# One decoder layer on one core: attention units in another order, outputs rounded one step earlier

## Chip, core and metric

The kernel runs on one core of one Trainium2 chip. The metric is the device time of one execution in microseconds. The core has five engines, each with an instruction queue of its own that is worked off strictly in order: TensorE (PE: matmuls and transposes), VectorE (DVE), ScalarE (ACT), GpSimd (POOL) and SyncE (SP, which only issues DMAs here). They wait for each other through semaphores: an instruction that ends adds to a counter, another engine's queue stands still until the counter has reached a number.

## What is computed

One layer of a decoder trunk on 512 tokens of width 1024. The change touches only the attention of the "native sparse" branch. Of the reference, cut to that part (16 heads of 64 channels, 4 key/value heads):

```python
def _nsa_branch(q, kv_cmp, kv_slc, kv_win, gate_logits, cmp_pos, cmp_w1, cmp_b1, cmp_w2, w_o):
...
        p_cmp = _masked_softmax(s, dist >= 0)
        o_cmp = jnp.einsum('bhgqn,bnhd->bqhgd', p_cmp, v_c)
...
        s = jnp.einsum('bqhgd,bkhd->bhgqk', qc, k_wc, preferred_element_type=jnp.float32) * scale
        s = s - slopes[:, :, None, None] * dist
        p = _masked_softmax(s, mask)
        o_win = jnp.einsum('bhgqk,bkhd->bqhgd', p, v_wc)
...
    o = jnp.einsum('zblhd,blhz->blhd', o, g)
    return o.reshape(bsz, L, Q_WIDTH).astype(q.dtype) @ w_o
```

`o` stacks the outputs of the compressed, the selected and the windowed branch; the selected one is computed like the windowed one, with its own keys and values, and g holds the gates.

With 512 tokens, 8 blocks of 64 and 8 blocks selected, both the selected and the windowed branch read every key up to the query (causal). So a tile of 128 queries needs 128, 256, 384 or 512 keys, for each head and each of these two branches.

## The kernel before

**Units.** The attention loop runs over 128 units (`UNITS`): 4 query tiles x 16 heads x 2 branches. `unit(u)` (line 95) gives for unit u the pair of heads m, the branch br, which head e of the pair, and the query tile qi; a unit reads n = 128 * (qi + 1) keys. Two units 2p and 2p + 1, the two heads of one m and br, are called a pair of units here. The order before is by query tile, longest first: units 0 to 31 have qi = 3 (512 keys), 32 to 63 have 384, 64 to 95 have 256, 96 to 127 have 128.

**Groups.** 16 units (8 pairs) are a group g: half of the heads for one query tile. Its values (64 channels x 128 queries for 8 heads) gather in one bank of PSUM, bank 4 or 5 by turns. When the last pair of the group is added, the result is rounded to its high part by ScalarE (`o_hi`, line 524, into hHi) and the remainder is taken by VectorE (`o_lo`, line 1148, into hLo, shown on line 890); both are operands of the output projection "nsa" that follows the loop. This is called the rounding of the group below.

**The software pipeline.** Every engine runs its own loop over u from 0 to 137, and step u handles several units of different age:

- TensorE: at even u the scores of units u and u + 1 (line 1697, `bank<-kqT` and `bank<-kS,kqT`; two heads side by side in the two halves of the rows); the transposes of unit u - 8 (`TURN`, line 1709, `bank<-ident,Sr`); at odd u the values of the pair u - 11, u - 10 (`PV`, lines 1725 to 1730): where br is 0 the compressed branch first (`bank<-PTc,Vbd`), then `bank<-PTr,VA`.
- VectorE: row minimum of unit u's scores, which writes Sr and nmax (line 1204); at odd u the inverse sums of the pair before (1214, 1215); at even u the copy of unit u - 8 from PSUM to PTr (1222).
- ScalarE: exp of unit u (683); at odd u the copy of unit u - 8 to PTr (691).
- POOL: scaling of unit u by inverse sum and gate (861).

Scores have three banks, transposes three, Sr ten buffers, PTr four. The rounding of a group stands in ScalarE's and VectorE's queues at the end of step u with u % 16 == 11 (`O_STEP`), an odd step, 13 steps after the first unit of the group's last pair; the last group's stands after the loop. Where it stands in ScalarE's code, and what TensorE waits for at the first pair of a later group, since its bank must be free:

```python
                if u % 16 == O_STEP and u > 16:
                    o_hi(act, (u // 16) - 1)
...
                    if w % 16 == 1 and w > 32:
                        pe.wait_ge(ohi_ready, w // 16 - 1)
                        pe.wait_ge(olo_ready, w // 16 - 1)
```

After the loop TensorE goes on with the projection "nsa" (line 1733), which needs the roundings of all groups: for its first four blocks of rows seven roundings, for the rest all eight. Its first weight tile is ready by then. Weights come through four buffers whose loads wait for TensorE's use; none is loaded during the loop.

Of the kernel before, what the change touches and what calls it, by code (L numbers as in the profile page):

```python
# [36 lines left out]
ACT = mybir.ActivationFunctionType  # L37
# [4 lines left out]
P = 128  # L42
# [8 lines left out]
NH, NKV, HD = 16, 4, 64  # L51
# [35 lines left out]
TURN, PV = 8, 10  # L87
RING = 10

O_STEP = 11  # L90

TURN_BANKS = (2, 3, 7)


def unit(u):

    return 4 * (u // 16 % 2) + u % 16 // 4, u // 2 % 2, u % 2, 3 - u // 32


_at = 0  # L100
# [8 lines left out]
def build(nc, I, out):  # L109
# [16 lines left out]
    hLo = at("hLo", [P, KT, T], 56 * KB, F32R)  # L126
# [73 lines left out]
    VA = at("VA", [P, 4, 512], RX + 32 * KB)  # L200
# [13 lines left out]
    Vbd = at("Vbd", [P, NKV, 4, HD], RX + 88 * KB)  # L214
    PTc = [at(f"PTc{i}", [P, NKV, P], RX + (94, 96, 48, 50)[i] * KB) for i in range(4)]
# [34 lines left out]
    with ctx:  # L250
        def sem(name):
            return ctx.enter_context(nc.semaphore(name))

        bank = [ctx.enter_context(nc.psum_tensor(f"bank{i}", [P, 512], F32)) for i in range(8)]
# [42 lines left out]
        score_done, max_done, exp_done, turned, turned_dve, turned_act, pv_done = (  # L297
            sem("score_done"), sem("max_done"), sem("exp_done"), sem("turned"), sem("turned_dve"),
            sem("turned_act"), sem("pv_done"))
# [3 lines left out]
        ohi_ready, olo_ready = sem("ohi_ready"), sem("olo_ready")  # L303
# [179 lines left out]
        def _(act):  # L483
# [38 lines left out]
                act.activation(rstd[:, :], rstd[:, :], ACT.Sqrt).then_inc(sd_ready, 1)  # L522

            def o_hi(a, g):

                a.wait_ge(pv_done, 16 * (g + 1))
                a.activation(hHi[:, 4 * (g % 2):4 * (g % 2) + 4, (3 - g // 2) * P:(4 - g // 2) * P],
                             bank[4 + g % 2][:, :].rearrange("p (k n) -> p k n", k=4), ACT.Copy).then_inc(ohi_ready, 1)

            def xo_hi(a, h):  # L530
                for dt in range(2):
# [39 lines left out]
            for ri in range(2):  # L571
                act.wait_ge(ct_turned, ri + 1)
                for q in range(2):
                    last = act.activation(Ct[64 * q:64 * q + 64, ri, :, :], bank[CT_BANKS[ri]][:, :].rearrange(
                        "p (g q c) -> p q g c", q=2, c=GC)[64 * q:64 * q + 64, q], ACT.Copy)
# [94 lines left out]
            for t in range(2, 8):  # L670
                c = BLOCKS["gmixc"] + t
# [6 lines left out]
            for u in range(UNITS + PV):  # L678
                if u < UNITS:
                    m, br, e, qi = unit(u)  # L680
                    n, h = P * (qi + 1), 2 * m + e
                    act.wait_ge(max_done, u + 1)
                    act.activation(Sr[u % RING][:, 0:n], Sr[u % RING][:, 0:n], ACT.Exp, bias=nmax[:, u % 8:u % 8 + 1],  # L683
                                   scale=-1.0, accum_out=sums[:, qi % 2, 1 + br, h:h + 1]).then_inc(exp_done, 1)
                v = u - TURN
                if 0 <= v < UNITS and v % 2 == 1:
                    n = P * (unit(v)[3] + 1)
                    act.wait_ge(turned, v + 1)
                    if v >= 4:
                        act.wait_ge(pv_done, v - 3)  # L690
                    act.activation(PTr[v % 4][:, 0:n], bank[TURN_BANKS[v % 3]][:, 0:n], ACT.Copy).then_inc(turned_act, 1)
                if u % 16 == O_STEP and u > 16:
                    o_hi(act, (u // 16) - 1)
            o_hi(act, 7)

            act.dma_start(memF[:, :, :], I["mem"][0].rearrange("(a p) n -> p a n", p=P)).then_inc(mem_landed, 16)
            for stage in ("nsa", "wx"):
# [33 lines left out]
            for n in range(4 * XH):  # L731
                h, qi = n // 4, n % 4
# [147 lines left out]
        def _(dve):  # L880
# [8 lines left out]
            def tt(o, a, b, op):  # L889
                return dve.tensor_tensor(o, a, b, op)  # L890
# [5 lines left out]
            for h in range(NH):  # L896
                half, m = slice(64 * (h % 2), 64 * (h % 2) + 64), h // 2
# [248 lines left out]
            dve.wait_ge(dist_ready, 1)  # L1146

            def o_lo(g):
                dve.wait_ge(ohi_ready, g + 1)
                dst = slice(4 * (g % 2), 4 * (g % 2) + 4), slice((3 - g // 2) * P, (4 - g // 2) * P)  # L1150
                tt(hLo[:, dst[0], dst[1]], bank[4 + g % 2][:, :].rearrange("p (k n) -> p k n", k=4),
                   hHi[:, dst[0], dst[1]].bitcast(F32), ALU.subtract).then_inc(olo_ready, 1)

            def compressed_scores(qi):
# [41 lines left out]
            for u in range(UNITS + PV):  # L1196
                if u < UNITS:
                    m, br, e, qi = unit(u)
                    n, h = P * (qi + 1), 2 * m + e
                    dve.wait_ge(score_done, u + 1)  # L1200
                    if u >= RING:
                        dve.wait_ge(turned, u - RING + 1)

                    dve.tensor_tensor_reduce(Sr[u % RING][:, 0:n], dist[:, T - n:T], bank[SCORE_BANKS[u % 3]][:, 0:n],  # L1204
                                             -SLOPES[h], 3e38, ALU.add, ALU.min, nmax[:, u % 8:u % 8 + 1]).then_inc(
                                                 max_done, 1)
                if u % 2 == 1 and 3 <= u < UNITS + 2:

                    m, br, e, qi = unit(u - 3)
                    p = u // 2 - 1  # L1210
                    dve.wait_ge(exp_done, u - 1)
                    if p >= 4:
                        dve.wait_ge(scaled, 2 * (p - 3))
                    link(dve.tensor_scalar(winv[:, p % 4, :], sums[:, qi % 2, 1 + br, 2 * m:2 * m + 2], 1e-30, None, ALU.max))
                    dve.reciprocal(winv[:, p % 4, :], winv[:, p % 4, :]).then_inc(winv_ready, 1)  # L1215
                v = u - TURN
                if 0 <= v < UNITS and v % 2 == 0:
                    n = P * (unit(v)[3] + 1)
                    dve.wait_ge(turned, v + 1)
                    if v >= 4:  # L1220
                        dve.wait_ge(pv_done, v - 3)
                    dve.tensor_copy(PTr[v % 4][:, 0:n], bank[TURN_BANKS[v % 3]][:, 0:n]).then_inc(turned_dve, 1)  # L1222
                if u % 16 == O_STEP and u > 16:
                    o_lo(u // 16 - 1)
            o_lo(7)


            b0 = BLOCKS["nsa"]
# [103 lines left out]
            for n in range(NX + XTURN + 1):  # L1332
# [4 lines left out]
                a = n - 1  # L1337
# [54 lines left out]
        def _(pe):  # L1392
            def mm(o, w, a, start, stop):
                return pe.matmul(o, w, a, start=start, stop=stop)  # L1394
# [294 lines left out]
            for u in range(UNITS + PV):  # L1689
                for v in (u, u + 1) if u < UNITS and u % 2 == 0 else ():  # L1690

                    m, br, e, qi = unit(v)
                    if v >= 3:
                        pe.wait_ge(max_done, v - 2)
                    half, kv = slice(64 * e, 64 * e + 64), m // 2
                    keys = kT if kv % 2 == e else kS
                    mm(bank[SCORE_BANKS[v % 3]][:, 0:P * (qi + 1)], qT[half, m, P * qi:P * qi + P],
                       keys[half, 2 * br + kv // 2, 0:P * (qi + 1)], True, True).then_inc(score_done, 1)
                v = u - TURN
                if 0 <= v < UNITS:  # L1700
                    qi = unit(v)[3]
                    pe.wait_ge(scaled, v + 1)
                    if v == 2:
                        pe.wait_ge(ptc_ready, 4)
                    elif v >= 3:
                        pe.wait_ge(turned_dve if v % 2 else turned_act, (v - 3) // 2 + 1)

                    for kt in range(qi + 1):
                        last = pe.transpose(bank[TURN_BANKS[v % 3]][:, P * kt:P * kt + P], Sr[v % RING][:, P * kt:P * kt + P],  # L1709
                                            ident[:, :])  # L1710
                    last.then_inc(turned, 1)
                w = u - PV
                if 0 <= w < UNITS and w % 2 == 1:

                    m, br, _, qi = unit(w)
                    pe.wait_ge(turned_dve, w // 2 + 1)
                    pe.wait_ge(turned_act, w // 2 + 1)
                    c, vcol = P * (m % 4), 256 * br + HD * (m // 2)
                    if w % 16 == 1 and w > 32:
                        pe.wait_ge(ohi_ready, w // 16 - 1)  # L1720
                        pe.wait_ge(olo_ready, w // 16 - 1)
                    if br == 0:

                        for e in range(2):
                            mm(bank[4 + w // 16 % 2][64 * e:64 * e + 64, c:c + P], Vbd[:, m // 2, (2 * m + e) % 4, :],
                               PTc[w // 32][:, m // 2, :], True, False)
                    for kt in range(qi + 1):
                        for e in range(2):
                            last = mm(bank[4 + w // 16 % 2][64 * e:64 * e + 64, c:c + P], VA[:, kt, vcol:vcol + HD],
                                      PTr[(w - 1 + e) % 4][:, P * kt:P * kt + P], False, br == 1 and kt == qi)  # L1730
                    last.then_inc(pv_done, 2)

# [215 lines left out]
```

## Time and profile before

| what | value |
|---|---|
| runs shown | 1177.78, 1169.0, 1169.27 us; median 1169.27 |
| the profiled execution: own time | 1168.06 us |
| its span, first to last instruction | 1166.3 us |
| mean granted TensorE clock | 0.991 |
| PE busy | 1128.6 us (97%) |
| DVE, ACT, POOL busy | 529.2, 435.6, 501.0 us (45, 37, 43%) |
| attention loop, first scores to last values | 362.31 to 515.09 us |

The span is the profiled execution's time less 1.8 us around it. A busy time is the union of an engine's instructions; matmuls are pipelined, so a busy TensorE isn't TensorE at its peak. In rows of the order of time the two fp32 passes of a matmul are rows or counts of their own, and "idle before" appears in brackets with the instruction that ended it.

### The profile page before, as it was taken

The numbers are of one execution on the slowest core, as the hardware profiler recorded it, in microseconds if no ns is written. First come the engines' busy times: TensorE is split into PE (matmuls) and PEld (weight loads), VectorE is DVE, ScalarE is ACT, GpSimd is POOL, SyncE is SP. The second block draws the span as 40 slices with busy tenths as digits, with TensorE's granted clock in tenths as the row PEclk, the third lists the DMA queues.
The fourth block names the chain that finished last, engine by engine and source line by source line (L and its number), as shares of the span: only waits on it lengthen the run. The fifth ranks groups of instructions, "written<-read, shape, count | busy, mean of one in ns | idle before, by whom it ended". The sixth has DMA issues, their size and how long they took to land.

```text
span 1166.3 us, 16854 instructions
## 1 busy us (share of the span) xinstructions
PE 1128.6 (97%) x6109; PEld 905.8 (78%) x6109; DVE 529.2 (45%) x1121; ACT 435.6 (37%) x766; POOL 501.0 (43%) x320
## 2 busy tenths in 40 slices
PE   6999999999999999999999999989999999999996
PEld 6878888887885666668887786767888888888885
DVE  7999912320157666756434816364222222310005
ACT  4341333311247667753324614236322322321211
POOL 5641451441134444554555640336444444434442
PEclk9998999999999999999999999999999999999999
DMA  6742331763031000013343430123333333323222
GB/s 192 93 106 69 91 108 39 249 163 89 22 82 43 1 2 2 1 56 90 109 120 124 139 106 19 58 87 108 91 93 105 90 98 100 90 73 108 91 92 89
DMA packets 158384, 101.68 MB, mean 87 GB/s; under 512 B 18344, under 2 KB 145968, under 8 KB 158192
## 3 DMA queue, kind: packets, MB, share of 16 engines
q1 hardware_dynamic: 153408, 94.48, 28.9%
q10 hardware_dynamic: 4912, 6.35, 1.6%
q8 instruction: 41, 0.67, 0.2%
q14 instruction: 23, 0.19, 0.1%
HBM read 93.59 MB, written 2.10 MB: 82 GB/s over the span
## 4 chain that ended last, share of the span: by engine, by line
PE 82%; DVE 7%; issue 5%; POOL 4%; ACT 2%; DMA 0%; POOLq 0%; DVEq 0%; ACTq 0%
PE bank L1394 78%; PE bank L1709 3%; POOL wlo L821 2%; DVE xc L890 1%; DVE Sr L1204 1%; POOL hLo L835 1%; DVE bank L1290 1%; DVE hLo L890 0%; DVE st L1374 0%; DVE bnst L909 0%; DVE xmax L1335 0%; ACT Wst L609 0%; DMA xtok<-in_x 0%; DVE xPT L1349 0%; DVE PTr L1222 0%
## 5 line engine op out<-in xcount | busy, mean ns | idle before, releaser
L821 POOL TENSOR_TENSOR wlo<-wraw,whi 128x1024 fp32r<-128x1024 f32 x160 | 393.4, 2460 | 519.5 <-ACT whi L498 519.3
L498 ACT ACTIVATE whi<-wraw 128x1024 fp32r<-128x1024 f32 x160 | 169.3, 1060 | 552.1 <-PE bank L1394 207.6
L1394 PE MATMUL bank<-hHi,whi 128*128 128x512 f32 x736 | 290.5, 395 | 8.6 <-ACT hHi L538 6.8
L1394 PE MATMUL bank<-hHi,wlo 128*128 128x512 f32 x736 | 288.4, 392 | 0.0
L1394 PE MATMUL bank<-hLo,whi 128*128 128x512 f32 x736 | 283.6, 390 | 0.0
L1394 PEld LDWEIGHTS bank<-hHi,whi 128*128 128x128 f32 x736 | 139.5, 190 | 40.5 <-ACT hHi L538 7.6
L1394 PEld LDWEIGHTS bank<-hHi,wlo 128*128 128x128 f32 x736 | 139.4, 189 | 29.3
L1394 PEld LDWEIGHTS bank<-hLo,whi 128*128 128x128 f32 x736 | 138.8, 189 | 28.4
L861 POOL TENSOR_SCALAR Sr<-Sr,winv,gates 128x512 f32<-128x512 f32 (+3 forms) x128 | 76.5, 607 | 78.6 <-DVE winv L1215 78.5
L890 DVE TENSOR_TENSOR sLo<-sF,sHi 128x512 f32 x22 | 50.1, 2275 | 99.3 <-ACT sHi L763 99.3
L683 ACT ACTIVATE Sr<-Sr,nmax 128x512 f32<-128x512 f32 (+3 forms) x128 | 71.7, 560 | 43.9 <-DVE nmax L1204 42.1
L1204 DVE CUSTOM_DVE_ANT_0 Sr<-dist,bank 128x512 f32<-128x512 f32 (+3 forms) x128 | 61.3, 481 | 32.3 <-PE bank L1394 32.0
L1394 PE MATMUL bank<-whi,sHi 128*128 128x512 f32 x176 | 68.6, 390 | 0.0
L1394 PE MATMUL bank<-wlo,sHi 128*128 128x512 f32 x176 | 68.5, 389 | 0.0
L1394 PE MATMUL bank<-whi,sLo 128*128 128x512 f32 x176 | 68.5, 389 | 0.0
L1374 DVE BATCH_NORM_STATS2 st<-bank 128x6 f32<-128x512 f32 x8 | 5.3, 689 | 111.7 <-PE bank L1394 111.7
L1709 PEld LDWEIGHTS bank<-ident,Sr 128*128 128x128 f32 x320 | 33.8, 141 | 25.7 <-POOL Sr L861 12.4
L1394 PE MATMUL bank<-kqT 64*128 64x512 f32 (+3 forms) x128 | 51.1, 481 | 0.8 <-DVE nmax L1204 0.7
L1394 PE MATMUL bank<-kS,kqT 64*128 64x512 f32 (+3 forms) x128 | 50.9, 482 | 0.0
L1709 PE MATMUL bank<-ident,Sr 128*128 128x128 f32 x320 | 49.0, 284 | 0.0
L1394 PE MATMUL bank<-PTr,VA 128*64 128x128 f32 x640 | 47.6, 278 | 0.0
L890 DVE TENSOR_TENSOR sF<-sg,bank 128x512 f32<-128x512 f32 x22 | 15.1, 687 | 71.6 <-ACT sg L770 63.2
(315 smaller groups left out, 1723.3 us busy)
## 6 DMA issues: line engine op xcount, KB each, us to landing
wraw<-in_ffn_w_in SPq DMA_DIRECT2D x88, 256.0 KB, 3.1
wraw<-in_w_in SPq DMA_DIRECT2D x80, 256.0 KB, 3.3
wraw<-in_ffn_w_out SPq DMA_DIRECT2D x44, 256.0 KB, 2.7
wraw<-in_xattn_w_kv SPq DMA_DIRECT2D x32, 256.0 KB, 3.1
w<-in_cmp_w ACTq DMA_DIRECT2D x1, 4096.0 KB, 20.1
wraw<-in_nsa_w_out SPq DMA_DIRECT2D x16, 256.0 KB, 3.1
wraw<-in_w_out SPq DMA_DIRECT2D x16, 256.0 KB, 3.1
wraw<-in_xattn_w_q SPq DMA_DIRECT2D x16, 256.0 KB, 3.1
```

Source lines behind the costliest of these rows:

```text
L498: act.activation(hi_of(c)[:, :], wraw[c % 4][:, :], ACT.Copy).then_inc(w_hi_ready, 1)
L683: act.activation(Sr[u % RING][:, 0:n], Sr[u % RING][:, 0:n], ACT.Exp, bias=nmax[:, u % 8:u % 8 + 1], scale=-1.0, accum_out=sums[:, qi % 2, ...
L821: pool.tensor_tensor(wlo[c % 4][:, :], wraw[c % 4][:, :], hi_of(c)[:, :].bitcast(F32), ALU.subtract).then_inc(w_lo_ready, 1)
L835: pool.tensor_tensor(hLo[:, m, :], hF[:, m, :], hHi[:, m, :].bitcast(F32), ALU.subtract).then_inc(hlo_ready, 1)
L861: pool.tensor_scalar(Sr[u % RING][:, 0:n], Sr[u % RING][:, 0:n], winv[:, u // 2 % 4, e:e + 1], gates[:, qi, 3 * h + 1 + br:3 * h + 2 + br] ...
L890: return dve.tensor_tensor(o, a, b, op)
L1204: dve.tensor_tensor_reduce(Sr[u % RING][:, 0:n], dist[:, T - n:T], bank[SCORE_BANKS[u % 3]][:, 0:n], -SLOPES[h], 3e38, ALU.add, ALU.min, n ...
L1290: link(dve.reciprocal(bank[7][:, :], rstd[:, :]))
L1374: last = dve.bn_stats(st3[:, a, half, :], bank[2 * a + half][:, :])
L1394: return pe.matmul(o, w, a, start=start, stop=stop)
L1709: last = pe.transpose(bank[TURN_BANKS[v % 3]][:, P * kt:P * kt + P], Sr[v % RING][:, P * kt:P * kt + P], ident[:, :])
```

## The change

The order of pairs comes from a list, `PAIRS`, of (group, pair in the group). Four 512-key pairs of group 0 come first; then 16 times a pair from the long list and one of the 16 shortest pairs (128 keys, groups 6 and 7) in turn, the long list being the other twelve 512-key pairs and the first four 384-key pairs of group 2; then the rest of group 2 and groups 3, 4 and 5 (384, 256, 256 keys). Groups end in the order 0, 6, 1, 7, 2, 3, 4, 5 (`ENDS`), at pairs 10, 19, 26, 35, 39, 47, 55 and 63. Groups 0, 1, 2 and 4 gather in bank 4, groups 6, 7, 3 and 5 in bank 5. `O_STEP` is 12 and now counts from the first unit of the group's last pair, so that a rounding stands at the end of an even step, one step earlier than before.

```diff
-O_STEP = 11
+O_STEP = 12
...
+LONG, SHORT = [(g, p) for g in (0, 1) for p in range(8)], [(g, p) for g in (6, 7) for p in range(8)]
+PAIRS = LONG[:4]
+for _i in range(16):
+    PAIRS += [(LONG + [(2, p) for p in range(4)])[4 + _i], SHORT[_i]]
+PAIRS += [(2, p) for p in range(4, 8)] + [(g, p) for g in (3, 4, 5) for p in range(8)]
+GROUP_END = {g: PAIRS.index((g, 7)) for g in range(8)}
+ENDS = sorted(GROUP_END, key=lambda g: GROUP_END[g])
+OUT_BANK = {0: 4, 6: 5, 1: 4, 7: 5, 2: 4, 3: 5, 4: 4, 5: 5}
+EARLIER = {1: 0, 7: 6, 2: 1, 3: 7, 4: 2, 5: 3}
...
 def unit(u):
 
-    return 4 * (u // 16 % 2) + u % 16 // 4, u // 2 % 2, u % 2, 3 - u // 32
+    g, p = PAIRS[u // 2]
+    return 4 * (g % 2) + p // 2, p % 2, u % 2, 3 - g // 2
+
+
+def finished(u):
+
+    return [g for g in ENDS if u == 2 * GROUP_END[g] + O_STEP]
...
-                a.wait_ge(pv_done, 16 * (g + 1))
+                out_bank = bank[OUT_BANK[g]]
+
+                a.wait_ge(pv_done, 2 * GROUP_END[g] + 2)
...
-                if u % 16 == O_STEP and u > 16:
-                    o_hi(act, (u // 16) - 1)
-            o_hi(act, 7)
+                for g in finished(u):
+                    o_hi(act, g)
+            o_hi(act, ENDS[-1])
...
-                dve.wait_ge(ohi_ready, g + 1)
+                dve.wait_ge(ohi_ready, ENDS.index(g) + 1)
...
-                if u % 16 == O_STEP and u > 16:
-                    o_lo(u // 16 - 1)
-            o_lo(7)
+                for g in finished(u):
+                    o_lo(g)
+            o_lo(ENDS[-1])
...
-                    if w % 16 == 1 and w > 32:
-                        pe.wait_ge(ohi_ready, w // 16 - 1)
-                        pe.wait_ge(olo_ready, w // 16 - 1)
+                    if first == 0 and g in EARLIER:
+                        pe.wait_ge(ohi_ready, ENDS.index(EARLIER[g]) + 1)
+                        pe.wait_ge(olo_ready, ENDS.index(EARLIER[g]) + 1)
```

The order that comes of it, on TensorE, from the scores of pair 8 of before (line 1394; the helper that records every matmul) and of pair 10 of the changed kernel (line 1412) on. `Sr` are the exponentials to be transposed, x4 being the four 128-key tiles of a unit; `PTr` are the copies of transposed tiles, `VA` the values. Before:

```order
L1394 MATMUL bank<-kqT 128x512
L1394 MATMUL bank<-kS,kqT 128x512
L1709 MATMUL bank<-ident,Sr_164 128x128 x4
L1709 MATMUL bank<-ident,Sr_165 128x128 x4
L1394 MATMUL bank<-PTc_176,Vbd 64x128 x2
L1394 MATMUL bank<-PTr_157,VA 64x128
L1394 MATMUL bank<-PTr_158,VA 64x128
```

And in the changed kernel:

```order
L1412 MATMUL bank<-kS,kqT 128x512
L1412 MATMUL bank<-kqT 128x512
L1727 MATMUL bank<-ident,Sr_166 128x128 x4
L1727 MATMUL bank<-ident,Sr_167 128x128 x4
L1412 MATMUL bank<-PTc_179,Vbd 64x128 x2
L1412 MATMUL bank<-PTr_159,VA 64x128
L1412 MATMUL bank<-PTr_160,VA 64x128
L1412 MATMUL bank<-kqT 128x128
L1412 MATMUL bank<-kS,kqT 128x128
L1727 MATMUL bank<-ident,Sr_168 128x128
L1727 MATMUL bank<-ident,Sr_169 128x128
L1412 MATMUL bank<-PTr_157,VA 64x128
```

Before, scores, transposes and values of one step pair are all of 512 keys (eight rows of values, two are shown). Now scores and transposes of a long pair are followed by the values of a short one (two rows in all), and scores and transposes of a short pair by the values of a long one (eight rows, one shown).

On ScalarE, around the first rounding (`hHi<-bank`), with the exponentials (`Sr,sums<-Sr,nmax`) and the copies (`PTr<-bank`). Before:

```order
L683 ACTIVATE Sr_171,sums<-Sr_171,nmax 128x512
L691 ACTIVATE PTr_160<-bank 128x512
L527 ACTIVATE hHi<-bank 128x4x128
L683 ACTIVATE Sr_172,sums<-Sr_172,nmax 128x512
L683 ACTIVATE Sr_173,sums<-Sr_173,nmax 128x512
L691 ACTIVATE PTr_158<-bank 128x512
```

And in the changed kernel:

```order
L709 ACTIVATE PTr_160<-bank 128x128
L701 ACTIVATE Sr_166,sums<-Sr_166,nmax 128x512
L545 ACTIVATE hHi<-bank 128x4x128
L701 ACTIVATE Sr_167,sums<-Sr_167,nmax 128x512
L709 ACTIVATE PTr_158<-bank 128x512
L701 ACTIVATE Sr_168,sums<-Sr_168,nmax 128x128
L701 ACTIVATE Sr_169,sums<-Sr_169,nmax 128x128
L709 ACTIVATE PTr_160<-bank 128x128
```

The rounding stood behind the copy of its pair of steps; it now stands between the two exponentials, ahead of the second one and of the copy. Exponentials and copies of 512 and of 128 keys now take turns.

## Rows read from the trace of the kernel before

**Rows 1.** Stretches of the loop: busy PE, PEld, DVE, ACT, POOL; PEclk, DMA, GB/s.

```profile
374.60:407.10 32.50, 32.20 (x302) 21.23 (x300) 22.04 (x71) 21.46 (x52) 15.12 (x21) 1.00 0.01 2
...
486.10:515.10 29.00, 27.38 (x259) 17.94 (x257) 19.21 (x120) 20.49 (x89) 16.15 (x36) 1.00 0.01 2
```

**Rows 2.** Order of time (start, duration), PE: first scores, first values, after the loop.

```profile
362.31 0.69 PE L1394 MATMUL bank<-kqT 64*128 64x512 f32 x1
...
373.36 0.44 PE L1394 MATMUL bank<-PTc,Vbd 128*64 128x128 f32 x4 [0.29 <-ACT PTr L691]
...
515.09 0.47 PE L1394 MATMUL bank<-hHi,whi 128*128 128x512 f32 x1
```

**Rows 3.** Order of time, 512-key laps: PE, DVE and ACT rows.

```profile
384.14 0.69 PE L1394 MATMUL bank<-kqT 64*128 64x512 f32 x1
...
385.20 1.09 PE L1709 MATMUL bank<-ident,Sr 128*128 128x128 f32 x8
...
386.52 0.68 DVE L1204 CUSTOM_DVE_ANT_0 Sr<-dist,bank 128x512 f32<-128x512 f32 x1
...
386.66 0.19 ACT L683 ACTIVATION_READ_ACCUMULATOR Sr<-Sr,nmax 128x1 f32 x1
...
387.47 0.69 PE L1394 MATMUL bank<-kqT 64*128 64x512 f32 x1
...
387.96 0.57 ACT L691 ACTIVATE PTr<-bank 128x512 f32<-128x512 f32 x1
...
389.55 1.09 PE L1394 MATMUL bank<-PTr,VA 128*64 128x128 f32 x16
390.57 0.69 PE L1394 MATMUL bank<-kqT 64*128 64x512 f32 x1
```

**Rows 4.** Order of time, lap after the first rounding: copy and values, ACT and PE.

```profile
405.17 0.58 ACT L691 ACTIVATE PTr<-bank 128x512 f32<-128x512 f32 x1
...
405.90 0.44 PE L1394 MATMUL bank<-PTc,Vbd 128*64 128x128 f32 x4 [0.30 <-ACT PTr L691]
```

**Rows 5.** Order of time, 384-key laps with the rounding of group 2: PE, ACT, DVE.

```profile
443.04 0.59 PE L1394 MATMUL bank<-kS,kqT 64*128 64x384 f32 x1
...
445.72 0.59 PE L1394 MATMUL bank<-kS,kqT 64*128 64x384 f32 x1
...
446.15 0.47 ACT L691 ACTIVATE PTr<-bank 128x384 f32<-128x384 f32 x1
446.52 0.58 ACT L527 ACTIVATE hHi<-bank 128x512 fp32r<-128x512 f32 x1
...
...
447.75 0.54 DVE L1204 CUSTOM_DVE_ANT_0 Sr<-dist,bank 128x384 f32<-128x384 f32 x1
...
449.88 0.47 ACT L691 ACTIVATE PTr<-bank 128x384 f32<-128x384 f32 x1
...
450.50 0.44 PE L1394 MATMUL bank<-PTc,Vbd 128*64 128x128 f32 x4 [0.43 <-ACT PTr L691]
```

**Rows 6.** Order of time, one 256-key lap: PE scores, the next lap's, ACT copy.

```profile
477.47 0.48 PE L1394 MATMUL bank<-kS,kqT 64*128 64x256 f32 x1
...
479.28 0.48 PE L1394 MATMUL bank<-kS,kqT 64*128 64x256 f32 x1
...
479.88 0.36 ACT L691 ACTIVATE PTr<-bank 128x256 f32<-128x256 f32 x1
```

**Rows 7.** Order of time, one 128-key lap on PE and the next one's scores.

```profile
502.26 0.37 PE L1394 MATMUL bank<-kqT 64*128 64x128 f32 x1
...
502.68 0.44 PE L1709 MATMUL bank<-ident,Sr 128*128 128x128 f32 x2
...
503.42 0.37 PE L1394 MATMUL bank<-kqT 64*128 64x128 f32 x1
```

**Rows 8.** Stretches around the one fall of the clock; columns as in rows 1.

```profile
84.00:88.00 4.00, 3.13 (x106) 3.13 (x108) 3.97 (x2) 2.08 (x5) 0.08 (x1) 1.00 0.00 0
...
96.00:100.00 4.00, 4.00 (x16) 3.71 (x17) 3.77 (x11) 0.00 (x0) 0.00 (x0) 0.50 0.01 2
```

More of the change, by code:

```diff
@@ L524, in o_hi @@
             def o_hi(a, g):
-                a.wait_ge(pv_done, 16 * (g + 1))
+                out_bank = bank[OUT_BANK[g]]
+                a.wait_ge(pv_done, 2 * GROUP_END[g] + 2)
                 a.activation(hHi[:, 4 * (g % 2):4 * (g % 2) + 4, (3 - g // 2) * P:(4 - g // 2) * P],
-                             bank[4 + g % 2][:, :].rearrange("p (k n) -> p k n", k=4), ACT.Copy).then_inc(ohi_ready, 1)
+                             out_bank[:, :].rearrange("p (k n) -> p k n", k=4), ACT.Copy).then_inc(ohi_ready, 1)
             def xo_hi(a, h):
@@ L1148, in o_lo @@
             def o_lo(g):
-                dve.wait_ge(ohi_ready, g + 1)
+                dve.wait_ge(ohi_ready, ENDS.index(g) + 1)
                 dst = slice(4 * (g % 2), 4 * (g % 2) + 4), slice((3 - g // 2) * P, (4 - g // 2) * P)
-                tt(hLo[:, dst[0], dst[1]], bank[4 + g % 2][:, :].rearrange("p (k n) -> p k n", k=4),
+                tt(hLo[:, dst[0], dst[1]], bank[OUT_BANK[g]][:, :].rearrange("p (k n) -> p k n", k=4),
                    hHi[:, dst[0], dst[1]].bitcast(F32), ALU.subtract).then_inc(olo_ready, 1)
@@ L1715, in _ @@
                     m, br, _, qi = unit(w)
+                    g, first = PAIRS[w // 2]
+                    out_bank = bank[OUT_BANK[g]]
                     pe.wait_ge(turned_dve, w // 2 + 1)
@@ L1718, in _ @@
                     c, vcol = P * (m % 4), 256 * br + HD * (m // 2)
-                    if w % 16 == 1 and w > 32:
-                        pe.wait_ge(ohi_ready, w // 16 - 1)
-                        pe.wait_ge(olo_ready, w // 16 - 1)
+                    if first == 0 and g in EARLIER:
+                        pe.wait_ge(ohi_ready, ENDS.index(EARLIER[g]) + 1)
+                        pe.wait_ge(olo_ready, ENDS.index(EARLIER[g]) + 1)
                     if br == 0:
                         for e in range(2):
-                            mm(bank[4 + w // 16 % 2][64 * e:64 * e + 64, c:c + P], Vbd[:, m // 2, (2 * m + e) % 4, :],
-                               PTc[w // 32][:, m // 2, :], True, False)
+                            mm(out_bank[64 * e:64 * e + 64, c:c + P], Vbd[:, m // 2, (2 * m + e) % 4, :],
+                               PTc[3 - qi][:, m // 2, :], True, False)
                     for kt in range(qi + 1):
                         for e in range(2):
-                            last = mm(bank[4 + w // 16 % 2][64 * e:64 * e + 64, c:c + P], VA[:, kt, vcol:vcol + HD],
+                            last = mm(out_bank[64 * e:64 * e + 64, c:c + P], VA[:, kt, vcol:vcol + HD],
                                       PTr[(w - 1 + e) % 4][:, P * kt:P * kt + P], False, br == 1 and kt == qi)
```

## The prediction

> **What bounds the kernel now.** I read three views, in this order: the busy time of each engine in stretches of the attention loop, the order of time of single laps of that loop on TensorE, VectorE and ScalarE, and the view of what ended each engine's idle time. Only the loop changes, so only it was read closely. I call two steps u = 2n and 2n + 1 lap n. In lap n TensorE issues the scores of pair n (S), the transposes of pair n - 4 (T) and the values of pair n - 5 (V, with four rows of the compressed branch, C, ahead of it when the pair's number in its group is even). VectorE does row minimum of unit 2n, copy of a transposed tile, row minimum of unit 2n + 1; ScalarE does exp(2n), exp(2n + 1), and last the other copy, on line 691. V of lap n + 1 needs that copy of lap n.
>
> TensorE is the bound in all of the loop: in the long stretch it is busy 32.20 of 32.50 us and in the shortest 27.38 of 29.00, while VectorE and ScalarE stay at about 70% in both [rows 1]. The laps show it as well: with 512 keys one lap takes 3.33 us with C and 3.10 without, S being 1.06, S and T together 2.08, V 1.02, C the difference, about 0.22 [rows 3]. With 384 keys it is 2.68 with C, so 2.46 without [rows 5]; with 256 keys 1.81 without C [rows 6]; with 128 keys 1.16 without, of which S is 0.42 and T and V the rest, 0.37 each [rows 7]; C adds its 0.22 to both. Sixteen laps of each kind, half of them with C, are 16 x (3.22 + 2.57 + 1.92 + 1.27) = 143.7 us of TensorE's own work. The loop takes 515.09 - 362.31 = 152.8 [rows 2]. So only 9.1 us are waits. Filling the pipe takes 2.65 of these: the first V comes 11.05 after the first S, against six S and two T of work, 8.40 [rows 2, 3]. The other 6.4 are the seven roundings inside the loop and small waits among the shortest pairs. This is all that a better order could win.
>
> What matters is how much slack hides the chain S, minimum, copy, minimum, exp, copy, V. With 512 keys the copy on line 691 starts 387.96 - 384.14 = 3.82 after its lap's S [rows 3], and where V has to wait it starts 0.73 after that copy's start [rows 4]. So V can't begin sooner than 4.55 after S of the lap before. In a row of long laps it begins at 389.55 - 384.14 = 5.41 after it [rows 3]: slack 0.86. With 384 keys the chain is 3.11 + 0.62 = 3.73 [rows 5].
>
> **The change, part by part.** Nothing is added or removed: the same instructions, DMAs, POOL scalings and queue orders outside the loop. Pairs change places, and each rounding moves ahead by one step.
>
> *Mixed laps.* In the mixed stretch an even lap is S long, T long, V short and an odd lap S short, T short, V long. TensorE's work from the even lap's S to the long V is now 2.08 + 0.37 (V short; 0.59 with C) + 0.42 + 0.37 = 3.24 or 3.46. The chain from that same S is unchanged in length, for its minima and exps are of the long pair and its copies of a long pair too, and none of the engines has a backlog: it is 4.55. So the slack of 0.86 becomes a wait of 1.31 or 1.09, once in every two laps, and nothing later takes it back, because the next long S is queued on TensorE behind the waiting V, and the next chain starts from it. Long laps 10 to 26 are nine such: 5 x 1.09 + 4 x 1.31 = 10.7. Lap 8 still has a long V in it, 3.89 of work against 4.55: 0.7. From lap 28 the long place holds 384-key pairs. Taking a third of 2.46 for each of their S, T and V, the same comparison with 3.73 (about 3.9 while 512-key tiles are still being copied) gives 0.9, 0.7, 0.9, 0.7, 0.5, 0.3 and 0 in laps 28 to 40: about 3.9. Together 15.3.
>
> *Filling.* Pair 5 is now short, which saves 0.64 of S before the first V, but that V waits for a copy on ScalarE whose place is unchanged; the work is conserved, so the wait grows: 0.6.
>
> *Roundings.* They stood after the copy of an odd step; now they stand between exp(2n) and exp(2n + 1) on ScalarE and between the two minima on VectorE. ScalarE could start one at 386.66 + 0.09 = 386.75, 2.61 after S; VectorE's half follows it, and the minimum behind that starts 447.75 - 446.52 = 1.23 after ScalarE's start [rows 3, 5]. The second minimum, normally at 386.52 or 2.38 [rows 3], so starts at 3.84: 1.46 late, and behind it stand exp(2n + 1), the copy and V. Group 0 (lap 16) and group 1 (lap 32) end where there is no slack: 1.46 each. Group 6 (lap 25) ends in a short lap, whose copy isn't wanted before 2.08 into the long lap after: 0. Groups 7 and 2 (laps 41, 45) fall among 384-key laps with slack 2.68 + 1.64 - 3.73 = 0.6: 0.9 each. Groups 3 and 4 fall among 256-key laps; their copy starts 479.88 - 477.47 = 2.41 after S [rows 6], V some 0.5 after that (0.73 and 0.62 for the two larger sizes), slack 2.03 + 1.21 - 2.91 = 0.3: 1.1 each. Sum 6.9 against the 6.4 that fall away with the old roundings and short waits. The first V of group 1 also waits now for group 0's rounding, one lap after it, but the copy it needs anyway comes later; cost 0. If that cover were gone it would be at most the 1.2 of the two roundings.
>
> *End.* The loop now drains with 256-key pairs; T and V there are TensorE work already counted, the last scaling on POOL comes well ahead of its T, and the last rounding stands where it stood. What follows (lines 1733 on) starts from the same state, later.
>
> Sum: 15.3 + 0.6 + 6.9 - 6.4 = +16.4 us. On the profiled execution's own 1168.06 this is 1184.5; it lies 1.2 under the median of the runs, 1169.27, so I forecast **1185.7 us**, 1.4% slower.
>
> **Rivals.**
> *Waits fill up (not slower).* If the short laps gave ScalarE and VectorE time to run ahead, so that the long copy is done when V is reached, no lap waits and even the 6.4 may go: 1162.9. For it: in every stretch both engines have 30% idle. Against: exp and minimum can't run ahead of an S that TensorE hasn't issued, and the 4.55 is latency from that S, not backlog. It decides only if the chain falls below 3.3 from 4.55. Chance 0.05. The Trainium skill, "Perfetto Trace Analysis", section "Optimization Strategy", says that where the most-contended engine changes over time, interleaving the regimes may help. The page speaks for this rival; by it the time would be near 1163. The profile of before doesn't meet its condition: the same engine is the fullest in all stretches.
> *Half hidden.* Each long V still waits, but by half (a shorter chain, copies that start early as the short copies leave the engines free) and the roundings overlap with it: +8, 1177. Chance 0.09.
> *The clock falls.* Waits of 1.1 to 1.3 in every 5.7 us could make the chip grant half the clock. It did once in this trace: 0.50 from 96 to 100 us, after a stretch in which TensorE was busy 3.13 of 4.00 us with small matmuls [rows 8]. In the mixed stretch TensorE would still be busy about 80% at full clock; should it run at half, the 4.5 us of work of a pair of laps double, 3.3 above my 5.7 per pair of laps, 14 times: +46, up to 1232. Against: in the shortest stretch the clock stayed 1.00 with waits at hand [rows 1]. Chance 0.04.
>
> **How the numbers follow.** The forecast has 0.80 and a range of its own of 1180 to 1191: the mixed term 15.3 could be 11 if each V starts 0.3 sooner (14 times), and the roundings could cost the 2 to 4 more that no slack would give. 0.02 is for what I haven't thought of. The range 1179 to 1192 leaves out the first rival, most of the second, the third, and a tenth of my own case. Of this kernel about 1% (11.7 us) can be told from no change. Faster by that much needs more than all the waits there are: 0.01. Within 1% (up to 1181.0): the first rival, most of the second and the edge of mine, 0.12. Slower: 0.87.
>
> **What would show it.** From the ninth lap on, the order of time should show long V starting about 4.5 us after S of the lap before, "idle" ahead of it ended by ScalarE's or VectorE's copy, and two laps taking 5.6 to 5.8 instead of 4.5. The loop should be about 169 us long, its 384- and 256-key laps of the later part unchanged at 2.46 to 2.68 and 1.81 to 2.03, and the stages behind it shifted as a block. Wrong would be: long V within 3.5 us of that S, granted clock under 1.00 in the mixed stretch, or waits at the first V of a group that VectorE's rounding ends.

## The result and the profile after

The changed kernel takes 1186.12 us in the median of four runs (1185.12 to 1188.07), the kernel before 1169.13 (1168.54 to 1177.78, four runs). The ratio is 1.014, 95% interval 1.0108 to 1.0173: 1.4% slower, and clear of no change. Forecast were 1185.7, 1179 to 1192. The profiled execution took 1185.12, 17.1 more than that of before.

The page of the changed kernel, its span, the first engines, and the granted clock in 40 slices:

```profile
span 1183.3 us, 16854 instructions
...
PE 1127.8 (95%) x6109; PEld 904.6 (76%) x6109; DVE 532.1 (45%) x1121; ACT 433.4 (37%) x766; POOL 500.5 (42%) x320
...
PEclk9998999999999999999999999998999999999999
```

TensorE is busy as long as before (1128.6 us then) and idle some 18 us more (55.5 against 37.7). The other engines' busy times change by 2.9 us at most. No work was added, TensorE waits.

The loop is where it waits. Order of time on TensorE (start, duration): first scores and first projection after the loop, as in [rows 2].

```profile
360.60 0.69 PE L1412 MATMUL bank<-kqT 64*128 64x512 f32 x1
...
531.37 0.50 PE L1412 MATMUL bank<-hHi,whi 128*128 128x512 f32 x1
```

That is 170.8 us against 152.8, +18.0. Ahead of the loop 1.7 us were saved by chance: the fall of the clock at 96 us [rows 8] was shorter. These stretches (columns as in [rows 1]) are of the changed kernel first, and second of the kernel before, where the clock was down earlier and was still down after 100 us:

```profile
94.00:98.00 4.00, 4.00 (x19) 3.95 (x19) 3.80 (x7) 0.00 (x0) 0.00 (x0) 0.50 0.01 2
98.00:102.00 4.00, 4.00 (x13) 3.16 (x12) 3.83 (x10) 0.00 (x0) 0.00 (x0) 0.65 0.00 0
102.00:106.00 4.00, 4.00 (x20) 3.29 (x19) 3.90 (x10) 1.12 (x2) 0.00 (x0) 1.00 0.31 78
```

```profile
92.00:96.00 4.00, 4.00 (x27) 4.00 (x26) 3.93 (x3) 0.00 (x0) 0.00 (x0) 0.66 0.00 0
...
100.00:104.00 4.00, 4.00 (x11) 3.12 (x11) 3.86 (x9) 0.00 (x0) 0.00 (x0) 0.56 0.04 8
```

What the granted clock lacks of 1.00 sums to (0.50 + 0.35) x 4 = 3.4 us in the changed kernel. In the kernel before, with the row from 96 to 100 us [rows 8], it sums to (0.34 + 0.50 + 0.44) x 4 = 5.1. The trace of before has falls that "the one fall of the clock" [rows 8] leaves out, outside the loop as well: one at 786 us, where TensorE was idle, and a last one near the end. The changed kernel has its like of the first of these at 804 us.

```profile
785.00:789.00 4.00, 0.00 (x0) 0.00 (x0) 3.97 (x4) 0.67 (x1) 0.00 (x0) 0.65 0.00 0
```

Behind the loop it is 0.8 more (652.0 from 531.37 to the end, against 651.2 from 515.09); why was not looked into. So 18.0 - 1.7 + 0.8 = 17.1.

The loop of the changed kernel in three stretches: filling and first laps, mixed laps, the rest.

```profile
361.00:384.47 23.47, 21.86 (x174) 13.40 (x170) 17.02 (x65) 15.74 (x47) 11.89 (x18) 1.00 0.05 13
384.47:461.50 77.03, 61.09 (x551) 39.39 (x549) 42.80 (x189) 40.50 (x134) 30.95 (x53) 0.98 0.00 1
461.50:531.40 69.90, 65.38 (x625) 43.25 (x623) 46.96 (x203) 47.41 (x148) 34.14 (x58) 1.00 0.01 2
```

In the mixed stretch TensorE, busy 99% of the long stretch in [rows 1], is idle for 16 of 77 us, and VectorE and ScalarE are less busy than before as well (56% and 53%). No engine is short of time; everyone waits for a chain.

Two laps of that stretch, TensorE, VectorE and ScalarE in the order of time:

```profile
384.47 0.69 PE L1412 MATMUL bank<-kS,kqT 64*128 64x512 f32 x1
...
386.85 0.68 DVE L1222 CUSTOM_DVE_ANT_0 Sr<-dist,bank 128x512 f32<-128x512 f32 x1
...
387.14 0.37 PE L1412 MATMUL bank<-kqT 64*128 64x128 f32 x1
...
387.56 0.44 PE L1727 MATMUL bank<-ident,Sr 128*128 128x128 f32 x2
387.57 0.72 ACT L701 ACTIVATE Sr<-Sr,nmax 128x512 f32<-128x512 f32 x1 [0.39 <-DVE nmax L1222]
...
388.29 0.58 ACT L709 ACTIVATE PTr<-bank 128x512 f32<-128x512 f32 x1
...
389.01 1.10 PE L1412 MATMUL bank<-PTr,VA 128*64 128x128 f32 x16 [1.01 <-ACT PTr L709]
390.04 0.69 PE L1412 MATMUL bank<-kqT 64*128 64x512 f32 x1
```

The copy on line 709 starts 388.29 - 384.47 = 3.82 after the long scores, exactly as in [rows 3], and the values 389.01 - 384.47 = 4.54 after them. TensorE had nothing to do from the end of the short transposes, 0.37 after 387.56, until then: 1.08 us. The next lap pair begins at 390.04, 5.57 after this one; a lap of each of these sizes took 3.22 + 1.27 = 4.5 before. The view of waits says the same in one line (us in total, times, longest): before, TensorE's matmuls waited 1.0 us in three places for ScalarE's copy; now, from 361 to 531 us,

```profile
PE bank L1412 <- ACT PTr L709: 19.4, 19, 2.6
```

### The profile page after: what moved, and what is told of

Its sections match the earlier page's. It is cut to its first block, busy times and chain, and to the rows that moved or that the text cites. A ratio compares the mean times of both kernels' runs of the same rounds, so it can differ in the third digit from the quotient of the medians.

```text
span 1183.3 us, 16854 instructions
## 1 busy us (share of the span) xinstructions
PE 1127.8 (95%) x6109; PEld 904.6 (76%) x6109; DVE 532.1 (45%) x1121; ACT 433.4 (37%) x766; POOL 500.5 (42%) x320
## 4 chain that ended last, share of the span: by engine, by line
PE 78%; DVE 8%; issue 7%; POOL 4%; ACT 3%; DMA 0%; POOLq 0%; DVEq 0%; ACTq 0%
PE bank L1412 76%; POOL wlo L839 2%; PE bank L1727 2%; DVE Sr L1222 2%; DVE xc L908 1%; POOL hLo L853 1%; ACT PTr L709 1%; ACT Sr L701 1%; DVE bank L1308 1%; DVE st L1392 0%; DVE bnst L927 0%; DVE hLo L908 0%; POOL Sr L879 0%; DVE xmax L1353 0%; ACT Wst L627 0%
## 5 line engine op out<-in xcount | busy, mean ns | idle before, releaser
L1412 PEld LDWEIGHTS bank<-PTr,VA 128*64 128x64 f32 x640 | 36.4, 137 | 16.2 <-DVE PTr L1240 9.1
```

## The experiments

The numbered ones are timed against the kernel before on the same chip (its median there 1168.5 to 1168.8). The ratio is formed over all runs of both kernels and need not be the quotient of the medians. "Loop" is from the first scores to the projection in one profiled execution; 143.7 of it is TensorE's own work. In four traces (after, e2, e5, e6) it holds a fall of the clock as well, which is priced where the run is told.

| kernel | order | change to it | median us | ratio, 95% interval | loop us |
|---|---|---|---|---|---|
| before | old | | 1169.13 | 1 | 152.8 |
| after | new | | 1186.12 | 1.014 (1.0108 to 1.0173) | 170.8 |
| e1_round_only | old | roundings one step earlier | 1170.48 | 1.0029 (0.9997 to 1.0062) | 154.4 |
| e2_mix_only | new | roundings at the old, odd step | 1184.66 | 1.0138 (1.0121 to 1.0155) | 168.8 |
| e5_mix_with_256 | new, 256-key pairs mixed in | | 1181.54 | 1.0105 (1.0083 to 1.0127) | 164.5 |
| e6_mix_with_384 | new, 384-key pairs mixed in | | 1170.94 | 1.0021 (1.0010 to 1.0032) | 157.2 |
| e3_new_order_pv12 | new | values a lap later | 1162.38 | 0.9948 (0.9932 to 0.9965) | 146.8 |
| e8_old_order_pv12 | old | values a lap later | 1164.11 | 0.9955 (0.9924 to 0.9986) | 149.0 |
| e4_new_order_copy_first | new | copy ahead of exp | 1163.55 | 0.9945 (0.9910 to 0.9981) | 148.0 |
| e7_old_order_copy_first | old | copy ahead of exp | 1163.42 | 0.9951 (0.9934 to 0.9968) | 148.1 |
| e9_new_order_both | new | both | 1162.73 | 0.9954 (0.9939 to 0.9969) | 146.6 |
| e10_old_order_both | old | both | 1163.36 | 0.9958 (0.9943 to 0.9973) | 148.0 |

**Which of the two parts.** The change has an order and a move of the roundings. Each alone:

```diff
-O_STEP = 11
+O_STEP = 10
```

> The kernel before with O_STEP 10 instead of 11: the order of pairs as before, each rounding one step earlier (between the two exps and between the two minima). My theory prices this by slack: 1.46 us late against a slack of 1.1 for group 0, 0.6 for the 384-key groups, 0.3 for the 256-key ones, about none for the 128-key ones, so 0.4 + 2 x 0.9 + 2 x 1.15 + 2 x 1.5 = 7.4 instead of 6.0: about +1.4, 1170.5 us. Rival A (the roundings are the main cost of the change): 1180 or more. Rival B (the earlier step helps, since an output bank is freed sooner): below 1168.5.

Measured: 1170.48, an interval that includes no change; loop +1.6, where +1.4 was expected. The matmuls behind each rounding waited 0.51 us among 512-key laps (group 0), 0.79 among 384-key laps (groups 1 and 2), 1.07 among 256-key (3 and 4), and 1.35 and 1.23 among 128-key laps (5 and 6): the shorter the units, the longer, as the cost of the chain would have it. Rival A falls, rival B has nothing for it.

```diff
-O_STEP = 12
+O_STEP = 13
```

> The changed kernel with O_STEP 13: the new order alone, roundings at the odd step as in the kernel before. My theory: the waits of the mixed laps stay (1.1 and 1.3 each), the two roundings that fall into mixed laps cost nothing, because the lap they now delay is a short one (-1.5 each), the others are 0.2 cheaper each, and the dip of the clock after the 2.7 us wait of lap 16 (some 1.6 us) goes with that wait: 1186.1 - 5.3 = 1181, with a granted clock of 1.00 through the mixed stretch. If the dip comes from the mix in general, it stays, 1182.5. If the roundings were the main cost: 1172 or less.

Measured: 1184.66, so the order alone costs nearly all of it, 1.38%. But my 1181 was 3.7 too low. Order of time around group 0's rounding, TensorE, ScalarE, VectorE:

```profile
405.96 0.44 PE L1727 MATMUL bank<-ident,Sr 128*128 128x128 f32 x2
...
406.91 0.58 ACT L709 ACTIVATE PTr<-bank 128x512 f32<-128x512 f32 x1
407.38 0.59 ACT L545 ACTIVATE hHi<-bank 128x512 fp32r<-128x512 f32 x1
...
408.00 0.69 DVE L908 TENSOR_TENSOR hLo<-bank,hHi 128x512 fp32r<-128x512 f32 x1 [1.57 <-ACT hHi L545]
...
408.84 0.44 PE L1412 MATMUL bank<-PTc,Vbd 128*64 128x128 f32 x4 [2.44 <-DVE hLo L908]
```

The copy didn't suffer, as I had said (the row puts TensorE's wait down to VectorE), but the values that come next are the first of group 1, which gathers in the bank that group 0 leaves. They wait for VectorE's half of the rounding, until 408.84, 1.2 longer than for the copy (406.91 + 0.73 = 407.64). In the changed kernel that half ends at 404.59 + 0.69 = 405.28, before the copy starts, and the wait is hidden:

```profile
404.59 0.69 DVE L908 TENSOR_TENSOR hLo<-bank,hHi 128x512 fp32r<-128x512 f32 x1 [0.76 <-ACT hHi L545]
...
406.64 0.58 ACT L709 ACTIVATE PTr<-bank 128x512 f32<-128x512 f32 x1
```

It is the same in the lap of group 1's rounding (a wait of 2.05 in e2, ended by VectorE's half too). So in the mixed order both places of the rounding cost 1.2 to 1.4, one through the exp, one through the bank. The clock fell here too, though after the later of the two waits: 0.54 from 454.6 to 458.0. The two laps behind took 5.50 us against 4.53 in the changed kernel, so this fall cost 1.0. With the two waits of 1.2 that is 3.4 of the 3.7.

```profile
454.60:458.00 3.40, 3.40 (x18) 1.90 (x16) 1.45 (x4) 0.93 (x4) 1.23 (x2) 0.54 0.00 0
```

**A dose.** If the cost is 4.55 minus TensorE's work in between, it must shrink with the size of what is mixed in. The edits exchange the groups in the list:

```diff
-LONG, SHORT = [(g, p) for g in (0, 1) for p in range(8)], [(g, p) for g in (6, 7) for p in range(8)]
+LONG, SHORT = [(g, p) for g in (0, 1) for p in range(8)], [(g, p) for g in (4, 5) for p in range(8)]
...
-PAIRS += [(2, p) for p in range(4, 8)] + [(g, p) for g in (3, 4, 5) for p in range(8)]
+PAIRS += [(2, p) for p in range(4, 8)] + [(g, p) for g in (3, 6, 7) for p in range(8)]
...
-OUT_BANK = {0: 4, 6: 5, 1: 4, 7: 5, 2: 4, 3: 5, 4: 4, 5: 5}
-EARLIER = {1: 0, 7: 6, 2: 1, 3: 7, 4: 2, 5: 3}
+OUT_BANK = {0: 4, 4: 5, 1: 4, 5: 5, 2: 4, 3: 5, 6: 4, 7: 5}
+EARLIER = {1: 0, 5: 4, 2: 1, 3: 5, 6: 2, 7: 3}
```

> The changed kernel with the 256-key pairs (groups 4 and 5) mixed among the long ones in place of the 128-key pairs, which now come last; banks follow. My theory: TensorE's work from a long lap's scores to the long values is 2.08 + 0.59 (0.81) + 0.63 + 0.59 = 3.89 or 4.11 against the chain's 4.55, so waits of 0.66 and 0.44 instead of 1.31 and 1.09; the nine long laps cost 5.0 instead of 10.7. With roundings of 7.6 and small waits: +7.4 over the kernel before, 1176.5 us (1178 if the clock dips after lap 16's wait again). If taking turns between sizes costs by itself, whatever the sizes: near 1186.

```diff
+LONG, SHORT = [(g, p) for g in (0, 1) for p in range(8)], [(g, p) for g in (2, 3) for p in range(8)]
...
+    PAIRS += [(LONG + [(4, p) for p in range(4)])[4 + _i], SHORT[_i]]
+PAIRS += [(4, p) for p in range(4, 8)] + [(g, p) for g in (5, 6, 7) for p in range(8)]
...
+OUT_BANK = {0: 4, 2: 5, 1: 4, 3: 5, 4: 4, 5: 5, 6: 4, 7: 5}
+EARLIER = {1: 0, 3: 2, 4: 1, 5: 3, 6: 4, 7: 5}
```

> The same with the 384-key pairs (groups 2 and 3) mixed among the long ones: 2.08 + 0.81 (1.03) + 0.85 + 0.81 = 4.55 or 4.77 of work against 4.55: no waits in the mixed laps outside the roundings. Roundings about 8.5 in all, 1171.5 us. If the mix costs by itself: 1180 or more.

With 256 keys, TensorE in the order of time, with the two copies that its values need:

```profile
387.36 0.69 PE L1412 MATMUL bank<-kS,kqT 64*128 64x512 f32 x1
...
389.14 0.69 DVE L1240 COPY PTr<-bank 128x512 f32<-128x512 f32 x1
...
390.89 0.66 PE L1727 MATMUL bank<-ident,Sr 128*128 128x128 f32 x4
391.18 0.57 ACT L709 ACTIVATE PTr<-bank 128x512 f32<-128x512 f32 x1
...
391.90 0.33 PE L1412 MATMUL bank<-PTr,VA 128*64 128x128 f32 x2 [0.36 <-DVE PTr L1240]
```

The last row names VectorE's copy, but that had ended at 389.83; the one that the values waited for is ScalarE's, again 3.82 after the scores. The values start at 391.90 - 387.36 = 4.54 again, and the short transposes' 0.59 leave a wait of 0.42; where the short values in between are without C it is 0.64. Expected were 0.44 and 0.66. With 384 keys the long values have none outside the roundings:

```profile
386.86 0.69 PE L1412 MATMUL bank<-kS,kqT 64*128 64x512 f32 x1
...
390.81 0.87 PE L1727 MATMUL bank<-ident,Sr 128*128 128x128 f32 x6
391.62 0.65 PE L1412 MATMUL bank<-PTr,VA 128*64 128x128 f32 x7
```

Here the values follow 0.81 after the transposes' start, which is what six transposes take, and 4.76 after the scores, past the 4.55. So 0, 0.42 to 0.64 and 1.08 to 1.29 us of wait for 384, 256 and 128 keys: taking turns between sizes costs nothing by itself. The total of e6 came as expected (1171.5, measured 1170.94), that of e5 was 5 us over (1176.5, measured 1181.54). Its trace has two falls of the clock, one in the lap of the long wait and one at the end of the loop, where the shortest pairs now stand:

```profile
412.00:416.00 4.00, 4.00 (x26) 2.16 (x24) 1.99 (x6) 0.81 (x2) 0.10 (x1) 0.66 0.00 0
516.00:520.00 4.00, 2.72 (x26) 1.72 (x28) 2.88 (x19) 3.00 (x15) 1.78 (x5) 1.00 0.00 0
520.00:524.00 4.00, 4.00 (x26) 2.32 (x28) 1.83 (x11) 1.95 (x10) 2.63 (x6) 0.57 0.02 4
524.00:528.00 4.00, 4.00 (x29) 2.51 (x26) 0.58 (x2) 0.72 (x4) 0.00 (x0) 0.58 0.00 0
```

Against the same phases at full clock they cost about 1.5 and 2.7 us. The loop was 11.7 longer than before; less these 4.2 it is 7.5, and 7.4 were forecast. e6's trace has a fall at the end too, worth 2.7: without it its loop would be 154.5, 1.7 above the one before. Its profiled execution took 1173.24, 2.3 over its median, and its ten runs reach from 1168.57 to 1173.84. So the agreement of the total is in part one of waits a little cheaper than forecast and a clock that the forecast left out.

**More slack, or a shorter chain.** Two edits attack the chain from its two ends and leave order, work and the placing of pairs alone. Values a lap later, with two more buffers (VectorE's copy and TensorE's values are changed in the same way, 4 to 6):

```diff
-TURN, PV = 8, 10
+TURN, PV = 8, 12
...
-O_STEP = 12
+O_STEP = 14
...
-    PTr = [at(f"PTr{i}", [P, T], RX + (40 + 2 * i) * KB) for i in range(4)]
+    PTr = [at(f"PTr{i}", [P, T], RX + (40, 42, 44, 46, 58, 60)[i] * KB) for i in range(6)]
...
-                    if v >= 4:
-                        act.wait_ge(pv_done, v - 3)
-                    act.activation(PTr[v % 4][:, 0:n], bank[TURN_BANKS[v % 3]][:, 0:n], ACT.Copy).then_inc(turned_act, 1)
+                    if v >= 6:
+                        act.wait_ge(pv_done, v - 5)
+                    act.activation(PTr[v % 6][:, 0:n], bank[TURN_BANKS[v % 3]][:, 0:n], ACT.Copy).then_inc(turned_act, 1)
...
```

> The changed kernel with the values one lap later (PV 12 instead of 10, six PTr buffers instead of four, O_STEP 14). Work and order are the same; only the slack behind the copy grows by a lap. If the cost of the change is the latency chain from scores to values, the waits in the mixed laps vanish and nearly all others too: loop about 147 us, 1163 to 1165 us, faster than both kernels. If the cost is throughput of ScalarE or VectorE, contention, the clock, or the output banks, more slack doesn't help: 1180 or more.

Measured: 1162.38, 2.0% under the changed kernel and 0.52% under the one before (interval 0.9932 to 0.9965). The loop is 146.8, as expected 147; the time lies a little under the 1163 to 1165 expected. Two mixed laps now:

```profile
386.94 0.69 PE L1412 MATMUL bank<-kqT 64*128 64x512 f32 x1
...
388.00 1.09 PE L1727 MATMUL bank<-ident,Sr 128*128 128x128 f32 x8
389.03 1.09 PE L1412 MATMUL bank<-PTr,VA 128*64 128x128 f32 x16
...
391.21 0.69 PE L1412 MATMUL bank<-kqT 64*128 64x512 f32 x1
```

4.27 us for the pair of laps, no "idle before" in any row. The granted clock stays at 1.00 through the loop. Throughput of ScalarE or VectorE, contention and the output banks would have left it at 1180 or more, by what was written before the run.

And ScalarE's copy ahead of the exp of the same step, with nothing else changed:

```diff
             for u in range(UNITS + PV):
-                if u < UNITS:
...
-                    act.activation(Sr[u % RING][:, 0:n], Sr[u % RING][:, 0:n], ACT.Exp, bias=nmax[:, u % 8:u % 8 + 1],
...
                 v = u - TURN
                 if 0 <= v < UNITS and v % 2 == 1:
...
+                if u < UNITS:
...
+                    act.activation(Sr[u % RING][:, 0:n], Sr[u % RING][:, 0:n], ACT.Exp, bias=nmax[:, u % 8:u % 8 + 1],
...
```

> The changed kernel with ScalarE's copy ahead of the exp of the same odd step instead of behind it. Buffers and distances as they are; the chain to the values no longer runs through the second minimum and the second exp. The copy can start when exp(2n) ends, 2.61 after the lap's scores, values 0.73 later at 3.34, against 3.24 or 3.46 of TensorE's work: waits of 0 to 0.1 per two laps instead of 1.1 and 1.3. Rounding in lap 16 costs about 0.5 instead of 2.8, and the fill gets shorter by up to 1.2. My theory: 1163 to 1166 us. If ScalarE were short of time rather than late: no gain, 1185.

Measured: 1163.55 (1163 to 1166 expected), loop 148.0. ScalarE and TensorE in one lap pair:

```profile
389.48 0.69 PE L1412 MATMUL bank<-kqT 64*128 64x512 f32 x1
...
392.09 0.58 ACT L703 ACTIVATE PTr<-bank 128x512 f32<-128x512 f32 x1
392.58 0.72 ACT L708 ACTIVATE Sr<-Sr,nmax 128x512 f32<-128x512 f32 x1
...
392.81 0.44 PE L1412 MATMUL bank<-PTc,Vbd 128*64 128x128 f32 x4
```

The copy starts 2.61 after the scores instead of 3.82 and the values 3.33 after them: the wait is 0.09. The exp that it overtakes starts at 392.58, 3.10 after the scores. That is when it started in the changed kernel too (387.57 - 384.47 in the two laps above), for there it had been waiting for the minimum. The step aside costs nothing. What is left are two waits of 0.7 for VectorE's half of a rounding, at the first values of groups 1 and 2, as in e2.

**Has the order a gain of its own, once the chain is hidden?** The same two edits in the old order, and both together in each:

> The kernel before with ScalarE's copy ahead of the exp of the same odd step. My theory: its only waits are roundings and the fill; the copy no longer stands behind the delayed minimum, so most of the 6.4 us go and the fill gets up to 1.2 shorter: 1162.5 to 1165 us, the same as the new order with this edit within 1.5 us, which would say that the order by itself has nothing left to give. If the new order had a gain of its own, the new order with this edit would be some 4 us or more below this one.

> The kernel before with the values one lap later (PV 12, six PTr buffers, O_STEP 13). My theory: waits of V at the roundings vanish, those of the scores behind a late minimum among the shortest pairs (about 0.8 each) stay: 1163.5 to 1166 us.

> The new order with both edits (values one lap later with six PTr buffers, and ScalarE's copy ahead of the exp). With the values a lap later the copy was hidden already, so my theory gives nothing more: the loop stays at about 146.8 us, which is TensorE's 143.7 and the fill, 1162 us. If some of the remaining 3.1 us hung on ScalarE's order: up to 1 us less.

> The old order with both edits. In the old order with the later values alone the loop took 149.0 us, because a rounding among the shortest pairs delays the minimum and with it the next scores (0.8 each, twice) and because of waits there of 0.1 to 0.2. My theory: these don't hang on the copy, so 148 to 149 us of loop and 1163.5 to 1164.5 in all, 1.5 to 2 above the new order with both. If the order has no gain of its own once the slack is there: equal within 0.5.

With the copy first the two orders are equal (1163.55 and 1163.42, loops 148.0 and 148.1); by the expectation for e7 the order then has nothing left to give. With the values later the new order has the shorter loop, 146.8 against 149.0; with both 146.6 against 148.0. In times that is 1.7 and 0.6 us. The expectation for e10 had 1.5 to 2 between the two kernels with both edits and "equal within 0.5" as its rival; 0.6 decides for neither. The intervals overlap in both cases (0.15 to 0.3% to either side, and 0.3% is 3.5 us), so the times leave it open; only the traces, one of each, show it. What e8 has left is at the shortest pairs, as expected, but its biggest piece is elsewhere than I had said: a transpose in the drain behind the rounding of group 6, waiting for a bank that VectorE empties late.

```profile
506.69 0.33 PE L1709 MATMUL bank<-ident,Sr 128*128 128x128 f32 x1
507.89 0.30 PE L1709 MATMUL bank<-ident,Sr 128*128 128x128 f32 x1 [0.87 <-DVE PTr L1222]
```

e3 and e9 have the lowest medians of all kernels here; between them nothing can be told (1162.38 and 1162.73). Their loops are 2.9 to 3.1 above TensorE's own work, most of it the fill.

## Why the prediction was right

*The bound and the reserve.* 143.7 us of work, 9.1 of waits and 2.65 of fill among them: the best loop of any kernel here is 146.6, 143.7 + 2.9. Of "all that a better order could win", 6.4 us, e3 won 6.0 in the loop, but by its slack together with the order; e8 won 3.8 with the old order and the same slack, and the order without slack lost.

*The chain.* Forecast were 4.55 us from scores to values; measured are 4.54 in the changed kernel, 4.54 in e5, and 3.33 when the second exp is out of it. That the short laps wouldn't let the other engines run ahead is shown by the rows: ScalarE and VectorE were idle, and the copy still came at 3.82.

*The terms* (the loop's +18.0, in the order of the forecast; measured from TensorE's start times):

| term | forecast | measured |
|---|---|---|
| 512-key mixed laps 8 to 26, without the rounding | 11.4 | 11.1 |
| 384-key mixed laps | 3.9 | 4.1 |
| filling | +0.6 | +0.6 |
| roundings | 6.9 | 6.8 |
| old roundings and small waits gone | -6.4 | -6.4 |
| drain | 0 | 0.3 |
| fall of the clock in the loop | 0 | 1.6 |
| sum | 16.4 | 18.1 |

The filling is exact for a reason: the first values come 371.65 - 360.60 = 11.05 after the first scores in both kernels, since ScalarE's queue up to there holds the same work. The term I had as a rival with 0.04, the clock, came in small. A granted clock under 1.00 in the mixed stretch also stands among the prediction's signs of being wrong, and it did come: 0.98 over the stretch. After the longest wait, that of lap 16's rounding (2.63 us idle), TensorE's clock was at its lower level for about 3 us. The wait, and the rows of it:

```profile
407.32 0.44 PE L1412 MATMUL bank<-PTc,Vbd 128*64 128x128 f32 x4 [2.63 <-ACT PTr L709]
407.56 1.52 PE L1412 MATMUL bank<-PTr,VA 128*64 128x128 f32 x16
...
409.01 1.22 PE L1412 MATMUL bank<-kqT 64*128 64x512 f32 x1
```

```profile
407.00:411.00 4.00, 3.68 (x24) 1.90 (x24) 0.17 (x1) 1.15 (x6) 1.68 (x3) 0.63 0.02 4
```

The scores' matmul, 0.69 elsewhere, takes 1.22 here. Values, scores and transposes of these laps took 1.6 more than their like. It is not the rival as I wrote it: it didn't stay, and the 1.1 to 1.3 us waits of the other laps didn't bring it on. Without it the loop is 16.4 longer, the forecast's own sum. That the whole time still came so near is luck in part: the profiled execution lost 1.6 here and saved 1.7 ahead of the loop.

*The parts apart.* The order alone gives 16.0 of the loop's 18.0 (e2), the roundings alone 1.6 in the old order (e1); the forecast had the mix at 15.3 + 0.6 and the move as 0.5 more than the old roundings. That 16.0 meets 15.9 so closely is chance: e2's 16.0 holds two waits for the bank (2.4) and a fall of the clock (1.0) that the forecast's mix has not, while its other roundings cost some 3 us less than the 6.4 of the old order. Of the bank the prediction says: "If that cover were gone it would be at most the 1.2". The size was right, 1.2 in e2; it was the expectation for e2 that left it out, though moving the rounding back takes this cover away.

*The rule on interleaving.* The Trainium skill, "Perfetto Trace Analysis", section "Optimization Strategy", says that interleaving regimes may help where the most-contended engine changes over time. No run here tests that case, for TensorE is the fullest engine in every stretch of [rows 1]. What the runs show is that interleaving without slack lost 1.4%. With the values a lap later it loses nothing, and the loop's trace is 1.4 to 2.2 us shorter than in the old order.

## What to carry to other kernels

In a software pipeline over units of several sizes the distance between stages is counted in units, but the latency it must cover is in microseconds. Before putting short units beside long ones, take the longest unit's chain from the trace and subtract the work of the bounding engine that will stand in that distance: what is missing is paid each time. Look also at what a late copy is queued behind: here it stood behind an exp that it doesn't need, and moving it ahead, a change of two statements, was worth about as much as a lap of buffers (1163.55 and 1162.38 us against 1186.12).

## What the hardware showed that was not expected

TensorE's granted clock fell to the lower of its two levels (1.2 instead of 2.4 GHz) for some microseconds inside the loop in four of the traces, five times in all, and in none of the other eight. In the changed kernel (0.63 from 407 to 411 us) it fell right after 2.63 us of idleness, in e5 at 412 us after a wait of 1.98. In e2 a wait of 2.44 us that ended at 408.8 passed without a fall, and one of 2.05 some 45 us later was followed by one. In e5 and in e6 it fell at the end, among the shortest pairs, a microsecond or so after a rounding's wait of 1.23. In e6:

```profile
500.00:511.00 11.00, 9.80 (x92) 6.09 (x88) 8.12 (x53) 8.61 (x39) 6.36 (x15) 1.00 0.00 1
511.00:519.00 8.00, 7.73 (x49) 4.63 (x50) 3.03 (x18) 3.30 (x15) 3.34 (x8) 0.58 0.01 2
```

In e1, with the same laps at the same end of its loop, TensorE had the same wait, and the clock stayed at 1.00 to the end of the loop:

```profile
511.34 0.40 PE L1394 MATMUL bank<-PTr,VA 128*64 128x128 f32 x3 [1.23 <-DVE PTr L1222]
```

So what decides it isn't settled by these runs. It cost 1.0 to 2.7 us each time, and each time it came behind a wait of 1.2 us or more, which is one more reason to avoid them.
